# Head-pair stage of a hybrid decoder step: values one slot behind their transposes, one burst of projections a slot, low parts of weights on VectorE

## The chip, the cores and the metric

The kernel runs on one core of one Trainium2 chip. The metric is the device time of one execution in microseconds. Five engines work side by side: TensorE (PE), VectorE (DVE), ScalarE (ACT), GpSimd (POOL) and SyncE (SP), which here issues nearly all DMAs in one queue. Each runs its own instructions in the order written, and they meet only in semaphores.

## The reference

One inference step of a one-layer decoder, for a prompt of 16 + 1024 tokens and 8 running sequences with 2048 cached positions each. Cut to what matters here:

```python
n = rms_norm(x, g_mix)
q, k, v, xr, gr, gates = split(n @ w_in)
z = einsum(q, k) / 8 + bias                       # 16 heads, 4 key/value heads
tail = cumsum_from_the_right(log_sigmoid(-z) shifted by one)
attn = einsum(exp(log_sigmoid(z) + tail), v)      # masked to earlier keys
xc = causal_conv4(xr); h = rg_lru(xc, gates r and i)
x = x + (sigmoid(ga) * attn + sigmoid(gb) * h * gelu(gr)) @ w_out
x = x + conv_ffn(rms_norm(x, g_ffn))
```

For the 8 running sequences the same attention goes over pages of 128 cached keys and values, found by a page table.

## The kernel before

`phase_mix` is the stage that the diff touches. Its loop runs over 8 turns `i`, one for each pair of query heads, which is also one column tile of 128 channels of the recurrent branch and one running sequence of the decode attention. All engines run the same 17 slots a turn, `slots(i, first)`. Slot `s` stands for one block of 64 prompt queries (`BLOCK_ORDER` alternates long and short ones: block b has 16 + 64 b keys).

For one block the work passes from engine to engine: `scores` (PE, into `p_z`), `score_out` (ACT, copies it twice, to `sums` and `z`), softplus by Exp and Ln (ACT), `positive`, `summing` (a scan) and `argument` (DVE), `weights` (ACT, Exp), `turn` (PE, transposes of up to four key blocks, into `p_wt`), `turn_out` (DVE, to `w_t`), `values` (PE, into `p_av`), `values_out` (DVE). `turn` and `values` of a block run LAG = 3 slots behind its scores. A block's key blocks come in one to three groups of four (27 groups a turn).

The gaps of this chain on PE are filled with projections, `project_piece`: four weight tiles (xr, ga, gr, gb) of three chunks of 350 columns, each as three matmuls for each of 8 contraction tiles (high times high, high times low, low times high), and six gate matmuls on `xc`. `spread` cuts these into 102 pieces, 6 a slot, and each slot's six into three places: one ahead of `decode`, one between the first and second group of values, one behind `scores(i, s + 1)`. The chunks alternate between the two halves of `p_proj`; ACT copies a finished chunk at the end of its slot (L942), and a chunk may start when the one two before it is copied (`proj_out`).

The weight tiles are split into a high part by ACT (`high_part`, L868, in slots 1, 4, 8 and 12) and a low part by POOL (`low_part`, L852).

The tail of the recurrent branch of pair i - 1 runs in turn i: ACT does it in slot 0 (L918 to L920, with two changes of its table), ahead of the softplus of slot 0; DVE has `gate` and `late` in slots 0 and 3 to 6, and `conv` in slots 4, 6, 7, 8 and 11.

`decode` of one sequence runs in the same slots: in slots 0 to 7 PE transposes a pair of key pages into `p_kt` (L1209), ACT copies them (L914), and PE makes their scores a slot later (L1198); DVE takes the scores up in slot 8 to 10; in slots 12 to 15 two value steps each (L1224), with the value page as the stationary operand and 8 weight columns moving, into two places.

SP's order is written out (L790 to L831): for each turn q of slots 0 and 1, page pairs 0 and 1, k_in (which waits for the last scores of the turn before), q of slots 2 and 3, weights, gate weights, and then for s = 0 to 14 a q load, the page pairs of `PAGES_AT`, and at s = 2 the four loads of v (which wait for the last values of the turn before). A page pair may be loaded when the pair two before it has been used (`page_used`). Each page load reads two page numbers from the table into registers first (L772).

## Time and profile before

| | us |
|---|---|
| median of 3 runs | 2318.98 |
| lowest, highest | 2315.67, 2320.23 |
| the profiled execution's own time | 2312.59 |
| its span, first to last instruction | 2310.9 |
| busy PE, PE weight loads | 2027.3, 1825.2 |
| busy DVE, ACT, POOL | 1216.0, 936.3, 330.4 |
| mean granted TensorE clock | 0.934 of full |

Up to about 205 us the kernel makes q, k and v; the head-pair stage runs to about 1300 us; the rest is the output projection and the feed-forward part, which the change doesn't touch. Busy times are sums over the span. A row of a time line gives the start and the length of one instruction, or of several alike (x8) merged; matmul records overlap, so that their starts tell the pace, not their lengths. In square brackets stands how long the engine had been idle before it, and what ended that. A clock of 0.50 is 1.2 GHz, one of 1.00 is 2.4 GHz.

### The profile page before, as it was taken

Reading aid. Unit: us, or ns where it says so; the run is one execution under the profiler, and the core shown is the slowest. Engines: PE = TensorE matmul, PEld = TensorE weight load, DVE = VectorE, ACT = ScalarE, POOL = GpSimd, SP = SyncE. Lnnn points to the kernel's source line nnn. Section 1 sums busy time; section 2 is a strip of 40 time slices with the busy share of each in tenths; the row PEclk is TensorE's granted clock in tenths of the full one; section 3 lists DMA queues with packets and bytes.
Section 4 is the critical chain, followed back from the end, with each engine's and each line's share of the span. In section 5 each row is a group of like instructions: output and inputs, shape, how many; then the busy total and the mean of one; then the engine's idle time right before and its main releaser. Section 6 shows DMA issues by size and latency. Waiting matters only on the chain. (4 is left out here: it accounts for less than half of the span.)

```text
span 2310.9 us, 42010 instructions
## 1 busy us (share of the span) xinstructions
PE 2027.3 (88%) x14708; PEld 1825.2 (79%) x14708; DVE 1216.0 (53%) x2023; ACT 936.3 (41%) x1498; POOL 330.4 (14%) x150
## 2 busy tenths in 40 slices
PE   4996998979898897989989598899999999999986
PEld 3896876767677686767778476799999999999985
DVE  6100645647465664747566634455545555455555
ACT  4111656565655756566475612222211222112213
POOL 4121100000010000001000300322212222122210
PEclk9998988989889898989989799899999999999998
DMA  3233322131322213132221221111111111111104
GB/s 118 87 89 90 83 66 63 48 82 47 85 64 57 72 48 83 47 84 65 63 66 51 77 95 73 45 55 46 40 33 54 45 45 36 36 54 45 45 19 162
DMA packets 206433, 148.23 MB, mean 64 GB/s; under 512 B 66485, under 2 KB 194550, under 8 KB 206228
## 3 DMA queue, kind: packets, MB, share of 16 engines
q1 hardware_dynamic: 206254, 145.99, 21.8%
q8 instruction: 94, 1.54, 0.3%
q14 instruction: 85, 0.70, 0.1%
HBM read 128.57 MB, written 17.61 MB: 63 GB/s over the span
## 5 line engine op out<-in xcount | busy, mean ns | idle before, releaser
L87 PE MATMUL d_p_up<-n_hi,d_w_hi 128*128 128x350 f32 x1056 | 343.7, 325 | 14.0 <-POOL d_w_lo L1563 7.7
L87 PE MATMUL d_p_up<-n_lo,d_w_hi 128*128 128x350 f32 x1056 | 342.8, 325 | 0.0
L87 PE MATMUL d_p_up<-n_hi,d_w_lo 128*128 128x350 f32 x1056 | 342.6, 324 | 0.0
L1710 DVE TENSOR_TENSOR mix<-mix,d_p_down 128x350 f32<-128x350 f32 x264 | 137.3, 520 | 320.7 <-PE d_p_down L1757 320.7
L87 PE MATMUL b_p_proj<-n_hi,b_w_hi 128*128 128x350 f32 x768 | 304.8, 397 | 0.0
L1607 ACT ACTIVATE d_up<-d_p_up 128x350 f32<-128x350 f32 x132 | 60.8, 462 | 499.5 <-PE d_p_up L87 499.5
L87 PE MATMUL b_p_proj<-n_lo,b_w_hi 128*128 128x350 f32 x768 | 260.9, 340 | 0.0
L87 PE MATMUL b_p_proj<-n_hi,b_w_lo 128*128 128x350 f32 x768 | 260.4, 339 | 0.0
L974 DVE COPY b_w_t<-b_p_wt 128x512 f32<-128x512 f32 (+5 forms) x216 | 119.2, 552 | 246.0 <-PE b_p_wt L1171 245.1
L852 POOL TENSOR_TENSOR b_w_lo<-w_raw,b_w_hi 128x1024 fp32r<-128x1024 f32 x33 | 82.5, 2501 | 960.1 <-ACT b_w_hi L868 960.1
L87 PEld LDWEIGHTS d_p_up<-n_hi,d_w_hi 128*128 128x128 f32 x1056 | 200.6, 190 | 15.0 <-POOL d_w_lo L1563 8.1
L87 PEld LDWEIGHTS d_p_up<-n_hi,d_w_lo 128*128 128x128 f32 x1056 | 200.6, 190 | 0.0
L87 PEld LDWEIGHTS d_p_up<-n_lo,d_w_hi 128*128 128x128 f32 x1056 | 200.4, 190 | 0.0
L1563 POOL TENSOR_TENSOR d_w_lo<-w_raw,d_w_hi 128x1024 fp32r<-128x1024 f32 x45 | 114.3, 2550 | 516.5 <-ACT d_w_hi L1593 516.5
L87 PEld LDWEIGHTS b_p_proj<-n_hi,b_w_hi 128*128 128x128 f32 x768 | 155.6, 203 | 39.6 <-issue 29.5
L1757 PE MATMUL d_p_down<-d_a_hi,d_wd_hi 128*128 128x350 f32 x480 | 157.9, 329 | 23.7 <-DVE d_a_lo L1701 23.7
L995 DVE TENSOR_TENSOR_SCAN b_sums<-b_sums 128x720 f32<-128x720 f32 (+16 forms) x136 | 169.7, 1247 | 13.7 <-ACT b_sums L929 13.6
L891 ACT ACTIVATE b_sums<-b_p_z,b_bias 128x720 f32<-128x720 f32 (+16 forms) x136 | 94.6, 696 | 160.3 <-PE b_p_z L1158 160.2
L1186 PE MATMUL b_p_av<-b_w_t,b_v_in 128*64 128x64 f32 (+1 forms) x1440 | 83.6, 251 | 84.6 <-DVE b_w_t L974 84.2
L87 PEld LDWEIGHTS b_p_proj<-n_lo,b_w_hi 128*128 128x128 f32 x768 | 156.5, 204 | 1.7
L1757 PE MATMUL d_p_down<-d_a_hi,d_wd_lo 128*128 128x350 f32 x480 | 157.1, 327 | 0.0
L1757 PE MATMUL d_p_down<-d_a_lo,d_wd_hi 128*128 128x350 f32 x480 | 156.5, 326 | 0.0
(241 smaller groups left out, 4138.1 us busy)
## 6 DMA issues: line engine op xcount, KB each, us to landing
w_raw<-in_w_in SPq DMA_DIRECT2D x45, 512.0 KB, 4.5
w_raw<-in_w_up SPq DMA_DIRECT2D x45, 512.0 KB, 3.7
b_page<-in_cache_k SPq DMA_DIRECT2D x128, 128.0 KB, 2.1
b_page<-in_cache_v SPq DMA_DIRECT2D x128, 128.0 KB, 2.1
w_raw<-in_w_down SPq DMA_DIRECT2D x22, 512.0 KB, 3.2
b_q_in<-q_scr SPq DMA_DIRECT2D x272, 32.0 KB, 2.2
q_scr<-a_q_stage SPq DMA_DIRECT2D x16, 260.0 KB, 3.4
b_k_in<-k_scr SPq DMA_DIRECT2D x16, 260.0 KB, 4.0
```

What stands on the lines that cost most here:

```text
L87: last = pe.matmul(out, w[:, k, :], x[:, k, col:col + CW], start=(k == 0 and w is w_hi and x is x_hi), stop=(k == KT - 1 and w is w_lo))
L852: pool.tensor_tensor(w_lo[:, slot, :, :], w_raw[:, slot, :, :], w_hi[:, slot, :, :].bitcast(F32), ALU.subtract).then_inc(w_lo_ready, 1)
L891: own.mark(act.activation(so, pz, ACT.Abs, bias=bias[:, 0:1]))
L974: dve.tensor_copy(w_t[0:rows, at, 0:here, :], p_wt[0:rows, 0:here, :]).then_inc(wt_out, 1)
L995: dve.tensor_tensor_scan(pos[:, ::-1], so[:, ::-1], pos[:, ::-1], 0.0, ALU.add, ALU.add)\
L1186: last = pe.matmul(p_av[HD * a:HD * (a + 1), 0:QB], v[0:size, m, :], w_t[0:size, at, r, QB * a:QB * (a + 1)], start=(n == 0 and r == 0), s ...
L1563: pool.tensor_tensor(w_lo[:, slot, :, :], w_raw[:, raw, :, :], w_hi[:, slot, :, :].bitcast(F32), ALU.subtract).then_inc(lo_ready, 1)
L1607: act.activation(up[:, u % 2, CW * c:CW * (c + 1)], p_up[:, n % 2, 0:CW], ACT.Copy).then_inc(up_out, 1)
L1710: dve.tensor_tensor(to, to, p_down[:, n % 4, 0:CW], ALU.add).then_inc(down_out, 1)
L1757: last = pe.matmul(p_down[:, n % 4, 0:CW], w[:, k, P * tile:P * (tile + 1)], a[:, k, CW * c:CW * (c + 1)], start=(k == 0 and w is wd_hi an ...
```

## The change

- PE: in each slot first all `values` of the block four slots back, then up to two `turn` of the block three back, then all six projection pieces in one go, further `turn`, `decode`, and `scores(s + 1)` at the end. The transposed weights get four buffers in `w_t` instead of two, and two in `p_wt` instead of one.
- DVE: `turn_out` stands behind `summing`; the low parts move here from POOL, to the ends of slots 1, 4, 8 and 12.
- Decode: everything about a slot later (`V_STEPS` 13 to 16, `PAGES_AT` 13 to 15); ACT's copy of a key page pair moves one slot on, directly behind `score_out`. The value steps now take the decode weights (16 heads and 16 columns of zeros) as the stationary operand and 256 page columns as the moving one, into four groups of 32 rows; DVE copies the sums (`decode_sum_out`), and PE adds and picks them with eight small matmuls against `pick` in slot 1 of the next turn.
- PSUM: scores take two banks and 16 columns of `p_kt` instead of three banks; `p_av`, `p_pick` and the decode scores share `p_misc`.
- SP: the same order, with the v loads at s = 3 and the slot loop one longer.
- After the loop the run-out is written in slots as well.

```diff
-V_STEPS = {12: (0, 1), 13: (2, 3), 14: (4, 5), 15: (6, 7)}
-PAGES_AT = {**{s: (s + 2,) for s in range(8)}, 12: (10, 11), 13: (12, 13), 14: (14, 15)}
+V_STEPS = {13: (0, 1), 14: (2, 3), 15: (4, 5), 16: (6, 7)}
+PAGES_AT = {**{s: (s + 2,) for s in range(8)}, 13: (10, 11), 14: (12, 13), 15: (14, 15)}
...
-                    for s in range(SLOTS - 2):
+                    for s in range(SLOTS - 1):
...
-                        if s == 2:
+                        if s == LAG:
                             sp.wait_ge(av_group, nth(i, GROUPS, GROUPS - 1))
...
                         score_out(i, s, first)
+                        if 1 <= s <= 8:
+                            act.wait_ge(page_used, nth(i, 16, s - 1, 2))
+                            act.activation(k_t[:, :, :].rearrange("p a c -> p (a c)"), p_kt[:, :],
+                                           ACT.Copy).then_inc(kt_out, 1)
                         if not first or s >= 2:
                             weights(i, s - 2)
...
+                def low_part(slot, index):
+                    dve.wait_ge(w_hi_ready, index)
+                    dve.tensor_tensor(w_lo[:, slot, :, :], w_raw[:, slot, :, :],
+                                      w_hi[:, slot, :, :].bitcast(F32), ALU.subtract).then_inc(w_lo_ready, 1)
...
                         if u >= 0 or not first:
                             positive(i, u)
-                        if groups:
-                            turn_out(i, v, 0)
-                        if u >= 0 or not first:
                             summing(i, u)
-                        if groups > 1:
-                            turn_out(i, v, 1)
+                        for n in range(min(groups, 2)):
+                            turn_out(i, v, n)
                         if u >= 0 or not first:
                             argument(i, u)
-                        if groups > 2:
-                            turn_out(i, v, 2)
-                        if s == SLOTS - 1:
-                            decode_values_out(i)
+                        for n in range(2, groups):
+                            turn_out(i, v, n)
+                        if s in W_AT:
+                            low_part((W_AT.index(s) + 1) % 2, nth(i, 4, W_AT.index(s) + 1))
...
+                def pick_heads(i):
+
+                    pe.wait_ge(vd_copied, nth(i, 1, 0))
+                    for kv in range(KVH):
+                        for odd in range(2):
+                            last = pe.matmul(p_pick[HD * odd:HD * (odd + 1), 2 * kv:2 * kv + 2],
+                                             vacc[:, HD * kv:HD * (kv + 1)],
+                                             pick[:, 4 * kv + odd:4 * kv + odd + 3:2], start=True, stop=True)
+                    last.then_inc(vd_picked, 1)
...
+                        for n in range(2):
+                            m = 2 * j + n
+                            last = pe.matmul(p_vd[32 * (m % 4):32 * (m % 4 + 1), :], zd_wide[:, :, m],
+                                             page[:, j % 2, n, :], start=(m < 4), stop=(m >= PAGES - 4))
...
-                        if groups:
-                            turn(i, v, 0)
-                        for n in range(3):
-                            for piece in PLACES[s][n]:
-                                project_piece(i, *piece)
-                            if n == 0:
-                                decode(i, s)
-                            if n < groups:
-                                values(i, v, n)
-                            if n + 1 < groups:
-                                turn(i, v, n + 1)
-                            if n == 1 and s + 1 < SLOTS:
-                                scores(i, s + 1)
+                        for n in range(len(key_groups(unit(v - 1)[0])) if v >= 1 or not first else 0):
+                            values(i, v - 1, n)
+                        for n in range(min(groups, 2)):
+                            turn(i, v, n)
+                        for piece in PLACES[s]:
+                            project_piece(i, *piece)
+                        for n in range(2, groups):
+                            turn(i, v, n)
+                        decode(i, s, first)
+                        if s + 1 < SLOTS:
+                            scores(i, s + 1)
```

## Rows read from the trace of the kernel before

**Rows 1.** Windows view, one pass: us; busy PE, PEld, DVE, ACT, POOL; clock; DMA share; GB/s.
```profile
614.80:750.82 136.02, 118.84 (x1037) 98.83 (x1038) 79.86 (x135) 81.43 (x133) 10.40 (x4) 0.90 0.24 64
```

**Rows 2.** The waits of 210 to 1300 us: total, times, longest.
```profile
PE b_p_av L1186 <- DVE b_w_t L974: 90.5, 42, 7.1
...
PE b_p_z L1151 <- DMA b_k_in<-k_scr: 37.8, 6, 19.1
```

**Rows 3.** Time line of TensorE: start, us, line, what; idle before it.
```profile
342.15 1.48 PE L1151 MATMUL b_p_z<-b_k_in,b_q_in 64*64 64x360 f32 x8 [2.53 <-DMA b_k_in<-k_scr]
...
750.82 1.33 PE L1151 MATMUL b_p_z<-b_k_in,b_q_in 64*64 64x360 f32 x8 [4.02 <-issue]
...
768.40 1.12 PE L1186 MATMUL b_p_av<-b_w_t,b_v_in 128*64 128x64 f32 x16 [7.05 <-DVE b_w_t L974]
...
784.54 0.69 PE L1186 MATMUL b_p_av<-b_w_t,b_v_odd 128*64 128x64 f32 x16 [1.15 <-DMA b_v_odd<-v_scr]
...
801.17 0.69 PE L1186 MATMUL b_p_av<-b_w_t,b_v_in 128*64 128x64 f32 x16 [2.26 <-DVE b_w_t L974]
...
828.75 0.69 PE L1186 MATMUL b_p_av<-b_w_t,b_v_in 128*64 128x64 f32 x16 [1.59 <-DVE b_w_t L974]
```

**Rows 4.** The time line of ScalarE, same columns.
```profile
737.17 0.44 ACT L942 ACTIVATE r_gb<-b_p_proj 128x350 f32<-128x350 f32 x1
...
755.29 0.60 ACT L914 ACTIVATE b_k_t<-b_p_kt 128x512 f32<-128x512 f32 x1 [0.71 <-PE b_p_kt L1209]
...
771.28 0.53 ACT L892 ACTIVATE b_z<-b_p_z,b_bias 128x336 f32<-128x336 f32 x1
```

**Rows 5.** The time line of TensorE, work without a wait.
```profile
728.62 0.59 PE L1224 MATMUL b_p_z<-b_zd,b_page 128*128 128x8 f32 x4
...
733.30 0.27 PE L1158 MATMUL b_p_z<-b_never,b_ident_b 64*64 64x64 bf16 x2
...
758.02 0.33 PE L87 MATMUL b_p_proj<-n_hi,b_w_hi 128*128 128x350 f32 x1
758.18 0.33 PE L87 MATMUL b_p_proj<-n_lo,b_w_hi 128*128 128x350 f32 x1
...
772.46 0.89 PE L1151 MATMUL b_p_z<-b_k_in,b_q_in 64*64 64x392 f32 x8
...
776.59 0.63 PE L1209 MATMUL b_p_kt<-ident,b_page 128*128 128x128 f32 x4
```

**Rows 6.** The time line of SP's DMA issues.
```profile
322.50 3.12 SPq L777 DMA_DIRECT2D b_page<-in_cache_v  x4
...
337.31 1.14 SPq L798 DMA_DIRECT2D b_k_in<-k_scr  x2
...
729.75 3.10 SPq L777 DMA_DIRECT2D b_page<-in_cache_v  x4
...
740.51 3.23 SPq L777 DMA_DIRECT2D b_page<-in_cache_k  x4
...
744.05 1.14 SPq L798 DMA_DIRECT2D b_k_in<-k_scr  x2
...
777.40 0.87 SPq L777 DMA_DIRECT2D b_page<-in_cache_k  x2
...
780.25 0.38 SPq L826 DMA_DIRECT2D b_v_odd<-v_scr  x1
```

**Rows 7.** The time lines of GpSimd and VectorE.
```profile
825.17 2.40 POOL L852 TENSOR_TENSOR b_w_lo<-w_raw,b_w_hi 128x1024 fp32r<-128x1024 f32 x1 [28.22 <-ACT b_w_hi L868]
...
825.30 2.80 DVE L988 TENSOR_SCALAR b_sums<-b_z 128x976 f32<-128x976 f32 x1
...
843.53 1.23 DVE L1001 TENSOR_TENSOR b_z<-b_z,b_sums 128x1040 f32<-128x1040 f32 x1
```

**Rows 8.** TensorE, the products nearest to the new value steps.
```profile
835.53 0.59 PE L1215 MATMUL b_p_kt<-b_spd,tri 128*128 128x256 f32 x2
835.96 0.59 PE L1216 MATMUL b_p_kt<-b_laterd,ones 128*128 128x256 f32 x2
```

More of the change, by code:

```diff
@@ L526, with w_t_before, p_wt_at, p_wt_before @@
 GROUPS = GROUPS_TO[-1]
+W_T_AT = (0, 1, 2, 3, 0, 1, 2, 3, 0, 1, 2, 3, 0, 1, 2, 3, 0, 1, 2, 3, 0, 1, 2, 3, 0, 1, 2)
+assert len(W_T_AT) == GROUPS
+def w_t_before(q):
+    return q - next(k for k in range(1, GROUPS) if W_T_AT[(q - k) % GROUPS] == W_T_AT[q % GROUPS])
+def p_wt_at(q):
+    return q % GROUPS % 2
+def p_wt_before(q):
+    return q - (2 if q % GROUPS else 1)
 def group_of(s, n):
@@ L549, in spread @@
         assert all(n < GATE_FIRST for n, _, _ in here) or s >= 12
-        a = (len(here) + 2) // 3
-        b = a + (len(here) - a + 1) // 2
-        places.append([])
-        for part in (here[:a], here[a:b], here[b:]):
-            place = []
-            for n, k0, k1 in part:
-                if place and place[-1][0] == n and place[-1][2] == k0:
-                    place[-1] = (n, place[-1][1], k1)
-                else:
-                    place.append((n, k0, k1))
-            places[-1].append(place)
+        place = []
+        for n, k0, k1 in here:
+            if place and place[-1][0] == n and place[-1][2] == k0:
+                place[-1] = (n, place[-1][1], k1)
+            else:
+                place.append((n, k0, k1))
+        places.append(place)
     assert at == len(pieces)
@@ L701, in phase_mix @@
         ident_b = sb("b_ident_b", [P, P], BF16)
-        w_t = sb("b_w_t", [P, 2, 4, P])
+        w_t = sb("b_w_t", [P, 4, 4, P])
         xr, xc, gr, gb, rg, ig, pc, rc = (branch.xr, branch.xc, branch.gr, branch.gb, branch.rg, branch.ig,
@@ L756, in phase_mix @@
         masks = sem("b_masks")
-        passed = [sem(f"b_passed{s}") for s in range(3)]
+        passed = sem("b_passed")
         w_view = g.w_in.rearrange("o (k p) c -> p (o k) c", p=P)
@@ L845, in _ @@
                                    pattern=[[-1, P]], channel_multiplier=1).then_inc(inits, 1)
-                for n, (part, value) in enumerate(((gate_w[:, :, :], 0.0), (xc[:, LAST:COLS], 0.0), (zd[:, :, :], 0.0), (spd[:, :, PAGES:PAGES + 1], 0.0))):
+                for n, (part, value) in enumerate(((gate_w[:, :, :], 0.0), (xc[:, LAST:COLS], 0.0), (zd_wide[:, :, :], 0.0), (spd[:, :, PAGES:PAGES + 1], 0.0))):
                     pool.wait_ge(inits, n + 2)
                     pool.memset(part, value).then_inc(inits, 1)
-                def low_part(slot, index):
-                    pool.wait_ge(w_hi_ready, index)
-                    pool.tensor_tensor(w_lo[:, slot, :, :], w_raw[:, slot, :, :],
-                                       w_hi[:, slot, :, :].bitcast(F32), ALU.subtract).then_inc(w_lo_ready, 1)
-                low_part(0, 1)
-                with pool.Fori(0, KT, 1) as i:
-                    for t in range(4):
-                        low_part((t + 1) % 2, nth(i, 4, t + 1))
             @block.scalar
@@ L1115, in _ @@
                     if s == 0:
+                        decode_sum_out(KT)
                         positive(KT, -1)
@@ L1221, in decode @@
                         pe.wait_ge(page_arr[j % 2], 32 * nth(i, 8, 4 + j // 2))
-                        for pair in range(2):
-                            for n in range(2):
-                                last = pe.matmul(p_vd[pair], page[:, j % 2, n, P * pair:P * (pair + 1)],
-                                                 zd[:, 8 * pair:8 * (pair + 1), 2 * j + n],
-                                                 start=(j == 0 and n == 0), stop=(j == 7 and n == 1))
+                        for n in range(2):
+                            m = 2 * j + n
+                            last = pe.matmul(p_vd[32 * (m % 4):32 * (m % 4 + 1), :], zd_wide[:, :, m],
+                                             page[:, j % 2, n, :], start=(m < 4), stop=(m >= PAGES - 4))
                         last.then_inc(page_used, 1)
@@ L1271, in _ @@
                     slots(i, False)
-                for v in range(-LAG, 0):
-                    for n in range(len(key_groups(unit(v)[0]))):
-                        turn(KT, v, n)
-                        values(KT, v, n)
+                for s in range(LAG + 1):
+                    for n in range(len(key_groups(unit(s - LAG - 1)[0]))):
+                        values(KT, s - LAG - 1, n)
+                    for n in range(len(key_groups(unit(s - LAG)[0])) if s < LAG else 0):
+                        turn(KT, s - LAG, n)
+                pe.wait_ge(av_out, nth(KT, SLOTS, -1, 1))
+                pick_heads(KT)
 def phase_out(nc, g, branch, sem):
```

142 lines of the change are left out of this document (82 added, 60 removed).

## The prediction

> **What bounds the kernel now.** The span is 2310.9 us. I read the stage of the eight head pairs (one turn of the loop is called a pass here), because the diff touches nothing else. By the windows view one pass takes 136.02 us, with TensorE busy for 118.84, VectorE for 79.86 and ScalarE for 81.43, at a granted clock of 0.90 [rows 1]. TensorE carries the stage, and the other two matter where it waits for them. The list of waits has two large ones on TensorE: 90.5 us for `b_w_t` and 37.8 us for `k_in` (19.1 of them before the first pass) [rows 2]. The time line of one pass places them [rows 3]: 4.02 us at the loop boundary, 7.05 in slot 1, 1.15 in slot 3 (`v_odd`), and 2.26, 1.59 and two under half a microsecond later. That is some 17 us a pass. I ask of each whether it goes, and what is late next.
>
> **The stall of slot 1 hardly moves.** It looks like a wait for `w_t`, but behind it stands ScalarE. Call T the start of `scores(0)`, 750.82. ScalarE copies scores 0, then runs the whole tail of the pair before, and only then `score_out(1)`, which ends at 771.28 + 0.53 = T + 21.0 [rows 4]. In the changed kernel TensorE no longer waits for `w_t` there, but at the end of slot 1 stand `decode` (it waits for the k_t copy that ScalarE now makes behind `score_out(1)`) and `scores(2)` (waits for `z_copied`). The copy of slot 0, with its wait, leaves ScalarE's path: 0.71 + 0.60 [rows 4]. So `k_t` is there at T + 21.0 - 1.3 + 0.5 = T + 20.2; eight score products and four transposes follow, some 2 us at the low clock, and `scores(2)` starts at T + 22.2. Before it started at 772.46 (T + 21.6), with 6 projection matmuls of the slot still to do, which start 0.16 us apart (758.02, 758.18) [rows 5]. The gain is about 0.5 us, not 7. TensorE idles there about as long as now.
>
> **The loop boundary gets longer.** `k_in` is reloaded each pass, behind the first two pages of the next pair in SP's queue. SP works there as one chain with no wait visible in it: pages 14 and 15 at 729.75, loop jump, q loads, pages 0 and 1 at 740.51, `k_in` at 744.05, TensorE on at 750.82 [rows 3, 6]. That is 21.1 us from the issue of page 14; at the first boundary it is 342.15 - 322.50 = 19.65. I take 20.7. The chain starts when value step 4 has released its page: 728.62 + 0.59 = 729.21, 0.54 before the issue [rows 5, 6]. Today 17.6 us of TensorE's work lie between that step and the end of the pass (750.82 - 4.02 = 746.80), so only 4 us show. The change moves step 4 from the first third of slot 14 to the end of slot 15. What is left behind it: step 5, `scores(16)`, values of 5 key blocks, their 5 transposes, 15 projection matmuls and one gate, and steps 6 and 7, which I price from the rows at 0.7 + 0.5 + 0.9 + 0.5 + 3.1 + 1.3 = 7.0 us [rows 3, 5, 8] (16 value records in 0.69, projections 0.16 each, scores 0.89 for 392 columns of which these have 200). The gap becomes 0.54 + 20.7 - 7.0 = 14.2 us instead of 4.0: **+10.2 at each of 7 boundaries, +71**. Bounds: if SP's chain had 3 to 4 us of hidden waiting in it, the gap still is at least 8.7 (pages 0 and 1 can't be issued before steps 6 and 7; from 740.51 to 744.05 is 3.5, and from 337.31 to 342.15, the least from `k_in` to scores, 4.8, and the pair of page releases is 0.4 apart), so +4.7 to +11.5. ScalarE and VectorE can't use this time: their slot 0 stands behind `scores(0)`.
>
> **The v loads get late.** SP issues them behind pages 5 (before: pages 4), which wait for the page transposes of slot 3 (before: slot 2). Before, those transposes ended at 777.22, the page loads went at 777.40, the last v load at 780.25, and TensorE went on at 784.54: 7.3 us [rows 3, 5, 6]. In the changed kernel only `scores(4)` (about 1 us) lies between the transposes and the values that want v, since decode now closes the slot and values open the next. The stall is 6.3 us instead of 1.1: **+5.2 in each of 8 passes, +42** (bounds 4.5 to 6).
>
> **One burst of projections waits for its own copy-outs.** `p_proj` has two buffers, and the copies stand at the end of ScalarE's slot. In slot 15 the gate matmul rg 2 follows its predecessor's end directly. Before, `scores(15)` ended at 733.57 and the copy of that buffer at 737.61, 4.0 us later [rows 4, 5]; the new order brings TensorE there after 0.3 of values, 0.5 of transposes and 1.2 of projection: a stall of 2.0. The same in slot 13: 0.4. In slot 12 the first gate wants `xc`, whose last convolution on VectorE stands behind the scan of 1040 columns and behind `td_done`, now a slot later: 1.0 (0 to 2). For VectorE's slots that are fuller than TensorE's (4 and 9) 0.6. Together **+4.0 a pass, +32** (1 to 6 a pass).
>
> **What goes.** The later waits for `w_t`, since the copy now has a slot of time: 90.5 less 7 times 7.05 is 41, of which some 5 stand in the run-out behind the loop [rows 2, 3]: **-36**. The slot 1 term: **-4**. Clock: a pass at 0.90 holds some 27 us at half clock [rows 1] (0.1 lost of 136, twice over); 16 value matmuls take 1.12 us there and 0.69 at full clock [rows 3]. Two of the stretches (behind the 2.26 wait, behind the products of 8 columns) may go: 2.3 a pass, **-18** (0 to -40). Two restarts of the projections less a slot, 0.1 us at each edge less what other operations pay among themselves: 2.0 a pass, **-16** (0 to -27). The value steps: 16 products of 256 columns instead of 64 short records; the nearest row has 0.43 for such a product (two records, from 835.53 to 835.96) [rows 8], 6.9 a pass in series against 7.1 now, less where neighbours in other column groups overlap, and 0.3 to 1.8 for picking heads: 0.8 a pass, **-6** (+12 to -24).
>
> **Low parts on VectorE.** 33 subtractions of 1024 columns. No row has this one on VectorE; the nearest is a subtraction of 1040 columns, 1.23 us [rows 7], so 4.9 us a pass on an engine that is busy for 79.86 of 136. In return a GpSimd low part no longer holds it: one ran from 825.17 for 2.40 us, and the VectorE instruction of 825.30 took 2.80, though it goes over fewer columns than the subtraction of 1.23 [rows 7]. It is part of why `w_t` was late in slots 5 and 9. The instruction waits for ScalarE's high part, and behind it on VectorE stand the next slot's copies; with a slot of slack for `w_t` I cost this at nothing. If that cover were gone it would be up to 1.2 us four times a pass, 39 in all.
>
> By itself: the Trainium skill (SBUF — State Buffer, section "SBUF: two separate sides") says GpSimd and a VectorE operation of two SBUF inputs or a two-port mode hold one shared pair exclusively; the row of 2.80 us agrees, and by it the move is a gain, not a cost.
>
> **Sum.** 71 + 42 + 32 = 145 added, 36 + 4 + 18 + 16 + 6 = 80 removed, 1 for a longer run-out after the loop: +66. The profiled execution took 2312.6 us, so 2378.6; the median of the runs is 6.4 above it, so **2385 us**, 2.9% slower.
>
> **Rivals.**
> The clock falls (0.15). The short operations, today spread between three bursts, now stand together: decode, scores, values, transposes make 3 to 3.5 us without a projection. If the clock fell in two slots of a pass at 1.5 us each, and the gain of 2.3 did not come, that is 24 + 18 = 42 more, 2427. For it: a pass holds 27 us of half clock already. Against: scores and values run at full clock elsewhere. By itself: the Trainium skill (TensorE: Matmul & The Clock Gate, section "Part 4: PE-mode transpose") says that transposes don't count as activity for the gate; no row here separates them, and by that rule this rival would be likelier.
> VectorE becomes the bound (0.08). The low part waits, and the copies of `w_t` and the values' copy behind it come late: 39 more, 2424. Against: 80 us of 136.
> SP's chain has slack (0.12). The boundary costs +4.7 instead of +10.2: 39 less, 2346.
> Faster (0.08). The loads land as they do today, because a slot of SP's queue ahead makes up for both shifts, and only what goes counts: 32 - 80 = -48 gives 2271. It decides from the point where the page of step 4 is released more than 17 us ahead of the pass's end. Against: the order of SP's queue is unchanged there, and its releases move later.
> The change doesn't do what it says, the stalls stay and the loads cost nothing (0.04): about 2319.
> My forecast: 0.53, its own range 2350 to 2415.
>
> **Range and chances.** 2340 to 2430 leaves out the faster case, the unchanged one and the worst of the clock. Within 0.2% is about what a measurement of this kernel can tell from no change. Faster 0.08, same 0.04, slower 0.88, by the cases.
>
> **What would show it.** A gap of 12 to 16 us before `scores(0)` on TensorE, released by `k_in`, and pages 0 and 1 issued after the pass's last matmul; one of about 6 us before `values(0)` released by v; 6 to 8 us left in slot 1, released by ScalarE's `k_t`; some 2 us before the gate matmul of slot 15; no wait for `w_t` above 1 us; low parts on VectorE near 1.2 us. A boundary gap under 9 us, a v stall under 3 or a slot 1 stall under 3 would make it wrong.

## The result, and the profile after

The changed kernel takes 2360.32 us (median of 4 runs, 2354.44 to 2367.18), beside 2317.32 for the kernel before: a ratio of 1.0188, 95% interval 1.0155 to 1.0220. It is 43 us slower; the forecast was 2385 us in a range of 2340 to 2430. The profiled execution took 2354.44 us with a span of 2352.7, 41.8 more than before. The six inner passes grew from 135.3 us on average (342.15 to 1153.92) to 140.6 (349.34 to 1192.97), which makes 32 of it; the first pass, up to the boundary at its end, is 8.9 longer, and the remaining 1 lies ahead of it and in the eighth and what follows.

Windows view of the changed kernel, one pass, with the columns of [rows 1]:

```profile
629.77:769.51 139.74, 108.47 (x1021) 91.88 (x1022) 78.78 (x134) 82.01 (x135) 0.00 (x0) 0.88 0.24 63
```

TensorE is busy 10.4 us less than in [rows 1], and the pass is 3.7 us longer (the passes differ; the mean of the six is 5.3 longer). The waits of TensorE, 205 to 1340 us (total, times, longest), show where it stands instead; the first two lines of [rows 2] are `L1219 <- DVE b_w_t` and `L1181 <- DMA b_k_in` here:

```profile
PE b_p_z L1181 <- DMA b_k_in<-k_scr: 115.4, 8, 18.9
PE b_p_misc L1219 <- DMA b_v_odd<-v_scr: 42.0, 8, 5.4
PE b_p_misc L1247 <- ACT b_k_t L923: 30.7, 7, 4.4
PE b_p_misc L1229 <- DVE mix L1006: 19.7, 8, 3.7
PE b_p_proj L1286 <- ACT r_gb L957: 16.7, 8, 2.1
PE b_p_misc L1219 <- DVE b_w_t L998: 15.6, 19, 2.8
PE b_p_proj L1286 <- issue: 14.5, 8, 1.8
```

The time line of TensorE, from the boundary at 769.51 to the next slot 15, answers to [rows 3]:

```profile
769.51 1.48 PE L1181 MATMUL b_p_z<-b_k_in,b_q_in 64*64 64x360 f32 x8 [13.84 <-DMA b_k_in<-k_scr]
...
784.89 0.63 PE L1229 MATMUL b_p_misc<-b_pick,b_posd 128*64 128x2 f32 x16 [2.18 <-DVE mix L1006]
...
789.96 1.87 PE L1247 MATMUL b_p_misc<-q_block,b_k_t 128*128 x8 [4.44 <-ACT b_k_t L923]
...
813.34 1.55 PE L1219 MATMUL b_p_misc<-b_w_t,b_v_odd 128*64 128x64 f32 x24 [5.27 <-DMA b_v_odd<-v_scr]
...
851.84 1.43 PE L1219 MATMUL b_p_misc<-b_w_t,b_v_in 128*64 128x64 f32 x32 [0.89 <-DVE b_w_t L998]
...
866.60 0.83 PE L1286 MATMUL b_p_proj<-r_xc,b_gate_w 128*128 128x350 f32 x2 [1.82 <-issue]
...
887.50 0.85 PE L1286 MATMUL b_p_proj<-r_xc,b_gate_w 128*128 128x350 f32 x2 [2.10 <-ACT r_gb L957]
```

The boundary has gone from 4.02 to 13.84, v from 1.15 to 5.27; the 7.05 of slot 1 has become 2.18 and 4.44; the waits of 2.26 and 1.59 for `w_t` are 0.89 and less; slots 12 and 15 have new ones of 1.82 and 2.10. For the 1.82 the profile names no releaser, but VectorE's last convolution ends at 866.50, 0.10 ahead of the gate matmul at 866.60 that reads its `xc`:

```profile
865.21 1.29 DVE L1051 SCALAR_TENSOR_TENSOR r_xc<-r_xr,r_pc,r_xc 128x1040 f32<-128x1040 f32 x1
```

SP's issues around the boundary, beside [rows 6]:

```profile
750.14 3.10 SPq L800 DMA_DIRECT2D b_page<-in_cache_v  x4
...
756.55 3.11 SPq L809 DMA_DIRECT2D b_q_in<-q_scr  x4
761.21 3.21 SPq L800 DMA_DIRECT2D b_page<-in_cache_k  x4
764.73 1.14 SPq L821 DMA_DIRECT2D b_k_in<-k_scr  x2
```

and TensorE's value steps 4 to 7 in that pass (two steps a row):

```profile
748.94 0.67 PE L1273 MATMUL b_p_kt<-b_page,b_zd 128*32 128x256 f32 x8
...
754.64 1.03 PE L1273 MATMUL b_p_kt<-b_page,b_zd 128*32 128x256 f32 x8
```

The row of steps 4 and 5 ends at 749.61, and the last pages go 0.53 later. From the issue at 750.14 to the scores at 769.51 it is 19.4 us of one chain through SP, and TensorE has work for the first 6 (to 755.67).

**Where the time went, by TensorE's own accounts.** Add up the distances from start to start on TensorE over a pass, less the idle time in brackets, and a pass falls into work and waiting. Single passes, named by their starts:

| us a pass | before, 614.80 / 884.46 | changed, 629.77 / 911.43 | e7, 633.91 |
|---|---|---|---|
| idle | 17.2 / 16.6 | 31.2 / 31.6 | 27.8 |
| work | 118.9 / 119.1 | 108.6 / 109.7 | 113.3 |
| of it 288 projection matmuls | 57.9 / 58.1 | 50.8 / 51.1 | 57.1 |
| value steps and picking heads | 7.1 / 7.1 | 3.7 / 4.3 | 5.1 |
| prompt scores | 11.3 / 11.9 | 10.0 / 10.0 | 10.0 |

Waiting rose by 14.5 us, work fell by 9.8. The change is slower because waiting rose by more.

One pass differs from the next by several us in how much of its work fell into stretches at half clock (13.7 to 20.0 us in the changed kernel, 16.8 to 28.0 before). So here are the means of all six inner passes, and beside them the work with the clock taken out. That is an estimate: projection matmuls in the middle of a burst start 0.29 us apart at half clock and 0.16 at full, so 0.45 of the work at half clock is taken off, for all kinds of work alike.

| us a pass, mean of six | before | changed | e7 |
|---|---|---|---|
| idle | 17.0 | 31.8 | 27.3 |
| work | 118.3 | 108.8 | 113.6 |
| of it at half clock | 20.9 | 16.4 | 18.6 |
| work without the clock | 108.9 | 101.5 | 105.3 |
| of it 288 projection matmuls | 53.4 | 48.9 | 54.8 |
| value steps and picking heads | 7.1 | 3.9 | 3.8 |
| prompt scores | 8.9 | 8.9 | 8.8 |

Waiting rose by 14.8 and work fell by 9.5: 7.4 by the order and form of the work, 2.0 by the clock (rounded). The estimate holds together: e3, e4, e9 and e10, with the changed order and unlike amounts of work at half clock, come to 101.5 to 101.9. The prompt scores are the same work at a better clock. The mean granted clock of the pass is lower all the same (0.88 against 0.90), since it counts the waiting too.

### The profile page after: what moved, and what is told of

Its sections match the earlier page's. It is cut to its first block and busy times, and to the rows that moved or that the text cites. A ratio compares the mean times of both kernels' runs of the same rounds, so it can differ in the third digit from the quotient of the medians.

```text
span 2352.7 us, 41657 instructions
## 1 busy us (share of the span) xinstructions
PE 1956.7 (83%) x14580; PEld 1775.2 (75%) x14580; DVE 1209.6 (51%) x2020; ACT 940.9 (40%) x1514; POOL 247.9 (11%) x117
## 3 DMA queue, kind: packets, MB, share of 16 engines
q1 hardware_dynamic: 206254, 145.99, 21.3%
## 5 line engine op out<-in xcount | busy, mean ns | idle before, releaser
L87 PE MATMUL b_p_proj<-n_hi,b_w_hi 128*128 128x350 f32 x768 | 272.9, 355 | 0.0
L87 PE MATMUL b_p_proj<-n_lo,b_w_hi 128*128 128x350 f32 x768 | 253.7, 330 | 0.0
L87 PE MATMUL b_p_proj<-n_hi,b_w_lo 128*128 128x350 f32 x768 | 253.0, 329 | 0.0
L1006 DVE COPY mix<-b_p_misc 128x64 f32 (+2 forms) x136 | 29.8, 219 | 350.9 <-PE b_p_misc L1219 344.6
L1181 PE MATMUL b_p_z<-b_k_in,b_q_in 64*64 64x360 f32 (+16 forms) x1024 | 103.2, 466 | 115.4 <-DMA b_k_in<-k_scr 115.4
L87 PEld LDWEIGHTS b_p_proj<-n_lo,b_w_hi 128*128 128x128 f32 x768 | 151.0, 197 | 2.2
L87 PEld LDWEIGHTS b_p_proj<-n_hi,b_w_lo 128*128 128x128 f32 x768 | 149.9, 195 | 0.0
```

The costliest lines, as they stand in the source:

```text
L87: last = pe.matmul(out, w[:, k, :], x[:, k, col:col + CW], start=(k == 0 and w is w_hi and x is x_hi), stop=(k == KT - 1 and w is w_lo))
L1006: dve.tensor_copy(g.mix[:, bass.ds(i if s >= 0 else i - 1, 1), FIRST + q0:FIRST + q0 + nq] .rearrange("p a c -> p (a c)"), p_av[:, 0:nq]). ...
L1181: last = pe.matmul(banks[bank][QB * a:QB * (a + 1), 0:k1 - k0], q_in[rows, Q_AT[s], a, :], k_in[rows, k0:k1], start=True, stop=k1 <= diagonal)
```

## The experiments

Each was timed beside the kernel before on the same chip, and ratios are to it; the changed kernel was timed in another batch, so a difference to it is taken through the ratios and through the medians. Lengths of passes are means of the six inner ones, from one profile of each kernel.

**e1: the v loads ahead of the pages, in slot 3 of the changed kernel.**

```diff
-                        for j in PAGES_AT.get(s, ()):
-                            load_pages(i, j)
                         if s == LAG:
                             sp.wait_ge(av_group, nth(i, GROUPS, GROUPS - 1))
...
+                        for j in PAGES_AT.get(s, ()):
+                            load_pages(i, j)
```

> The changed kernel with SP's four v loads of slot 3 issued ahead of page pair 5. Theory (v comes late because its loads stand behind the page transposes of slot 3): the wait for v_odd, 5.1 to 5.4 us in each pass, falls under 1 us; 8 x 4.5 to 5.2, 36 to 42 us less than the changed kernel, so about 2320, ratio to before near 1.00. Rival (the wait is only slack that shows there; ScalarE and VectorE are as late): the gap moves to a wait for w_t or z in slots 4 to 6 and the time falls by less than 15 us.

2331.43 us, 1.0081 (1.0054 to 1.0108), some 27 us less than the changed kernel (25 by the ratios, 29 by the medians). TensorE's wait:

```profile
661.19 0.92 PE L1219 MATMUL b_p_misc<-b_w_t,b_v_odd 128*64 128x64 f32 x24 [1.45 <-DMA b_v_odd<-v_scr]
```

5.3 has become 1.45, 3.8 us eight times or 30, nearly all of it in the time (11.1 us of waiting for v are left of 42.0). The wait is caused by the place in SP's queue; the forecast of 36 to 42 assumed that it goes entirely.

**e2: `k_in` first in SP's pass; e3: both.**

```diff
+                    sp.wait_ge(qk_done, nth(i, SLOTS, SLOTS - 1))
+                    for half in range(2):
+                        sp.dma_start(k_in[HD * half:HD * (half + 1), :], g.k_scr[bass.ds(group, 1), :, :]
+                                     .rearrange("a p c -> p (a c)")).then_inc(k_arr, 16)
                     load_q(i, 0)
                     load_q(i, 1)
                     load_pages(i, 0)
                     load_pages(i, 1)
-                    sp.wait_ge(qk_done, nth(i, SLOTS, SLOTS - 1))
-                    for half in range(2):
-                        sp.dma_start(k_in[HD * half:HD * (half + 1), :], g.k_scr[bass.ds(group, 1), :, :]
-                                     .rearrange("a p c -> p (a c)")).then_inc(k_arr, 16)
```

> The changed kernel with SP's k_in loads as the first thing of a pass, ahead of q of slots 0 and 1 and of pages 0 and 1. Theory (the boundary is SP's chain): the gap before scores(0), 13.5 to 13.9 us, falls to about 6.3 (SP is back from its jump some 0.9 us after the pass's last matmul, and 5.4 from the k_in issue to the scores), so 7 x 7.5 = 53 us less, about 2307. Rival (TensorE's own jump and the landing of q take as long): the gap stays above 10, under 25 us less.

> Both orders of SP changed. If the two waits add up: 89 to 95 us less than the changed kernel, about 2267, ratio to before about 0.978: faster than both kernels. Rival (one wait hides the other, or they give way to ScalarE): less than 75% of the two gains together.

e2: 2314.38 us, 0.9996 (0.9978 to 1.0014), some 45 us less than the changed kernel. e3: 2281.42 us, 0.9863 (0.9830 to 0.9896), some 77 less; the two gains (27 and 45) add. The 53 and the 89 to 95 that were expected are missed, because neither wait went as far as forecast. The boundary in e2 and in e3:

```profile
614.36 1.48 PE L1181 MATMUL b_p_z<-b_k_in,b_q_in 64*64 64x360 f32 x8 [7.56 <-DMA b_q_in<-q_scr]
```

```profile
728.69 1.48 PE L1181 MATMUL b_p_z<-b_k_in,b_q_in 64*64 64x360 f32 x8 [6.99 <-DMA b_q_in<-q_scr]
```

The wait has halved and changed its releaser: behind `k_in` the q loads were next. With the boundary wait halved the changed kernel is level with the one before, with v shortened too it is ahead. These two waits are what makes it slower.

**e9: e3, with the next pass's q(0), q(1) and `k_in` issued ahead of SP's loop jump** (the last pass is written out behind the loop).

```diff
+                        if s in (12, 13) and more:
+                            load_q(i + 1, s - 12)
...
+                    if more:
+                        load_k(i + 1)
+
+                load_k(0)
+                load_q(0, 0)
+                load_q(0, 1)
+                with sp.Fori(0, KT - 1, 1) as i:
+                    one_pass(i, True)
+                one_pass(KT - 1, False)
```

> Both orders of SP as in the kernel with both loads ahead, and the next pass's q of slots 0 and 1 and k_in issued before SP's loop jump (k_in behind page 15, some 2.4 us ahead of the pass's last matmul). Theory: the gap before scores(0), 7.0 us there, falls to TensorE's own jump or k_in's landing, 3 to 4.5 us: 7 x 2.5 to 4 = 18 to 28 us less than 2281, about 2258. Rival (something else holds 7 us, such as SP's other loads behind it): under 8 us less.

2272.04 us, 0.9810 (0.9785 to 0.9834), 9 to 12 less than e3 where 18 to 28 were expected.

```profile
722.11 1.48 PE L1194 MATMUL b_p_z<-b_k_in,b_q_in 64*64 64x360 f32 x8 [3.82 <-issue]
```

The gap fell from 7.0 to 4.2 in the mean of the six (3.8 in this row), but a pass only from 130.3 to 129.4. What the boundary gives is lost again elsewhere: the work that TensorE does at half clock rose from 15.8 to 19.1 us a pass, and 0.45 of that rise is 1.5 of the missing 1.9 us. Why the clock fell more often isn't shown. The gap that is left isn't all TensorE's own, either, though the profile names no releaser: the second `k_in` load was issued at 716.37 and took 4.2 to land, so it landed at 720.56, 2.3 us after TensorE's last matmul had ended (718.28).

**e6 and e11: SP's order alone, in the kernel before.** e6 has the edit of e2; e11 also has the v loads ahead of the q load and the pages of slot 2.

> The kernel before with k_in as SP's first load of a pass; it waits there for the scores of slot 16, some 5.5 us ahead of the pass's end. k_in is then in place before the pass ends. Theory A (TensorE's own jump back takes near 4 us): the gap stays at 3.5 to 4.4 us and the time within 8 us of before. Theory B (k_in is what it waits for): the gap falls under 2 us, 14 to 28 us faster. Rival: q or the key pages come late now and the gap or slot 0 grows, slower.

> The kernel before with both edits of SP's order: k_in first in the pass, and the v loads of slot 2 ahead of that slot's q load and key pages. It tells how much of the time saved in the changed kernel by the same two edits (which took it from 2360 to 2281) the old order of work could have had too, and so what the new order of TensorE is worth once SP no longer holds it up. Theory (the new order gains by itself: projections and value steps faster, later waits for w_t gone): here only the boundary (worth 10 alone) and the v stall of 1.15 x 8 = 9 can go, so 2293 to 2301 us, ratio 0.990 to 0.994, and the kernel stays 12 to 20 us above the 2281 of the changed order with the same edits. Rival (the new order is worth nothing, the same edits give the same): 2285 or less, ratio 0.987 or below.

e6: 2303.32 us, 0.9956 (0.9939 to 0.9972). e11: 2289.79 us, 0.9898 (0.9876 to 0.9921). For e6 neither theory held: the gap fell to 2.2 to 2.7 us (A said 3.5 to 4.4, B under 2), and the time by 11 us. At the boundary there is a gap which no load ends:

```profile
739.43 0.83 PE L1151 MATMUL b_p_z<-b_k_in,b_q_in 64*64 64x360 f32 x8 [2.19 <-issue]
```

There `k_in` had landed a microsecond before TensorE's last matmul ended. The first boundary, where TensorE comes from the first turn, written out ahead of the loop, and doesn't jump back, has no such gap:

```profile
339.37 0.53 PE L1151 MATMUL b_p_z<-b_k_in,b_q_in 64*64 64x360 f32 x4 [0.47 <-DMA b_q_in<-q_scr]
```

So some 2.2 of the 4.02 in [rows 3] were TensorE's own jump, and only 1.8 were `k_in`. e11 lies below its forecast of 2293 to 2301 and above the rival's 2285. With like edits on SP the changed order (e3) has 0.9863 against 0.9898: ahead by 8 us, though the two intervals overlap, where I had expected 12 to 20. The new order is worth less by itself than its work suggests: of the six inner passes, e3 has 108.9 us of work against 116.0 in e11, but 21.3 of waiting against 15.7, above all since it still waits 6.99 at the boundary, where the old one waits 2.3.

**e7: the changed kernel with the six projection pieces of a slot in three places again** (before further `turn`, behind `decode`, behind `scores`).

```diff
-                        for piece in PLACES[s]:
+                        for piece in PLACES3[s][0]:
                             project_piece(i, *piece)
                         for n in range(2, groups):
                             turn(i, v, n)
                         decode(i, s, first)
+                        for piece in PLACES3[s][1]:
+                            project_piece(i, *piece)
                         if s + 1 < SLOTS:
                             scores(i, s + 1)
+                        for piece in PLACES3[s][2]:
+                            project_piece(i, *piece)
```

> The changed kernel with each slot's projection pieces in three places again (2 behind the transposes, 2 behind decode, 2 behind the next scores); values, transposes, copies and loads as changed. It sizes the one burst. As predicted (2.0 us a pass for the restarts, 4.0 lost to copy-outs in slots 12 to 15): the restarts come back, +16, the waits for the copy-outs mostly go, -20: within 15 us of the changed kernel. By the pace in the traces (288 projection matmuls took 57.9 us of a pass before and 51.3 after): if the burst makes all of that, +50 - 20, 20 to 35 us slower than changed; if the clock makes it, the pace stays at 51 to 53 us a pass and the time falls.

2361.88 us, 1.0198 (1.0175 to 1.0221): within 0.1% of the changed kernel. The tables above tell why that is a sum of two: over the six passes work is up by 4.8 and idle time down by 4.5. The same 288 matmuls take 57.1 us instead of 51.0 in the single passes, and 54.8 instead of 48.9 with the clock taken out. The trace has 47 bursts a pass in e7 (gate matmuls counted in) and 17 in the changed kernel, so 30 more breaks cost some 5.9 us, 0.20 each. The time came out as forecast, but by luck: the restarts cost 5.9 us a pass and not 2.0, and 4.5 less waiting (forecast 2.5) and 1.4 less for the transposes of key pages made up for it. The boundary shows one piece of it:

```profile
633.91 1.48 PE L1193 MATMUL b_p_z<-b_k_in,b_q_in 64*64 64x360 f32 x8 [12.04 <-DMA b_k_in<-k_scr]
```

Where TensorE waits for a chain elsewhere, slower work of its own costs nothing. Against e7's three places one burst is worth 6 us a pass, and as long as SP sets the boundary a good part of it isn't collected. Against the three places of the kernel before it is worth less: 53.4 to 48.9, some 4.4 us for 34 fewer bursts (51 to 17), 0.13 each. At full clock a projection matmul inside a burst starts 0.160 after the one before it in all three kernels; to the next start it takes 0.26 to 0.28 for the first of a burst, and for the last 0.20 before, 0.19 in the changed kernel and 0.24 in e7. So the price of a break depends on what follows it.

**e4, e5, e12: the low parts.** e4 is the changed kernel with `low_part` on GpSimd, e5 the kernel before with it on VectorE (at the ends of slots 1, 4, 8 and 12), e12 the fastest kernel (e10, below) with it on GpSimd. Each moves the same block, `low_part` and its calls; e5 in the direction opposite to the one shown:

```diff
-                def low_part(slot, index):
-                    dve.wait_ge(w_hi_ready, index)
-                    dve.tensor_tensor(w_lo[:, slot, :, :], w_raw[:, slot, :, :],
-                                      w_hi[:, slot, :, :].bitcast(F32), ALU.subtract).then_inc(w_lo_ready, 1)
+                def low_part(slot, index):
+                    pool.wait_ge(w_hi_ready, index)
+                    pool.tensor_tensor(w_lo[:, slot, :, :], w_raw[:, slot, :, :],
+                                       w_hi[:, slot, :, :].bitcast(F32), ALU.subtract).then_inc(w_lo_ready, 1)
```

> The changed kernel with the low parts of the projection weights back on GpSimd; all else as changed. My step priced this part at nothing, because w_t has a slot of time: within 6 us of the changed kernel (ratio to before 1.016 to 1.022). Rival (VectorE's low part is what keeps the w_t and xc waits, 0.9 + 0.6 + 1.8 us a pass): up to 15 us faster than changed. Rival (GpSimd holds VectorE for 2 us where it counts): slower by more than 10 us.

> The kernel before with one part of the change alone: the low parts on VectorE, at the ends of its slots 1, 4, 8 and 12. If GpSimd's 2.4 us hold on VectorE is part of why w_t came late (2.26 and 1.59 us in slots 5 and 9), those waits shrink by 1 us or more each and the time falls by 5 to 20 us (with the low parts back on GpSimd the changed kernel was 13 us slower). Rival (no slack for w_t in this order, so VectorE's own 1.23 us and its wait for the high part delay the transposes' copies): 10 to 30 us slower, with longer waits for w_t.

> The fastest kernel so far (2241 us, ratio 0.967) with the low parts of the weights back on GpSimd. In the changed kernel this alone cost 13 us, with the waits nearly the same and more time at the half clock. Theory A (GpSimd's 2.4 us operations slow VectorE's work, and TensorE's clock pays for it wherever VectorE is late): about 10 to 15 us slower here too, ratio 0.971 to 0.974. Theory B (the 13 us were the clock's reaction to the long idle stretches at the boundary and before values(0), which are gone here): within 5 us, ratio 0.965 to 0.969.

| | ratio (interval) | the part on VectorE against GpSimd |
|---|---|---|
| e4 | 1.0256 (1.0223 to 1.0290) | 12 to 16 us faster |
| e5 | 1.0077 (1.0053 to 1.0101) | 18 to 20 us slower |
| e12 | 0.9638 (0.9619 to 0.9657) | 7 to 11 us slower (the intervals of e10 and e12 overlap a little) |

In e5 the rival held, in e12 neither theory. In e4 the time is that of the last rival, but its mechanism isn't what happened, as the next rows show. The sign of the effect depends on the rest of the kernel.

The hold by GpSimd is real in the kernel before, where a GpSimd low part always met this instruction of VectorE; it is gone in the changed kernel, and does not come back in e4 (groups by form in the kernel before, the changed one and e4: total busy, mean ns, idle before):

```profile
L988 DVE TENSOR_SCALAR b_sums<-b_z 128x976 f32<-128x976 f32 x8 | 22.5, 2808 | 0.0
L1013 DVE TENSOR_SCALAR b_sums<-b_z 128x976 f32<-128x976 f32 x8 | 5.3, 660 | 0.0
L1016 DVE TENSOR_SCALAR b_sums<-b_z 128x976 f32<-128x976 f32 x8 | 5.2, 655 | 0.0
```

The sum of all VectorE instructions but the low parts tells what the hold costs VectorE in a pass: 85.4 before against 81.1 in e5, so 4.2; 80.6 in e4 against 80.2, so 0.4; 82.7 in e12 against 80.3 in e10, so 2.4. The time goes the other way: where the hold was largest, moving the low parts to VectorE cost most, and where there was next to none, it gained. e5 can be read. On VectorE the instruction itself is as priced, but it waits for ScalarE's high part (groups of VectorE: total busy, mean ns, idle before):

```profile
L958 DVE TENSOR_TENSOR b_w_lo<-w_raw,b_w_hi 128x1024 fp32r<-128x1024 f32 x33 | 40.4, 1226 | 73.0 <-ACT b_w_hi L858 73.0
```

(the changed kernel's low parts wait 29.1 in all), and behind it stand the copies of `w_t`, which have no slot of slack in the old order. TensorE in e5:

```profile
675.87 0.73 PE L1186 MATMUL b_p_av<-b_w_t,b_v_in 128*64 128x64 f32 x16 [3.19 <-DVE b_w_t L972]
...
704.75 0.69 PE L1186 MATMUL b_p_av<-b_w_t,b_v_in 128*64 128x64 f32 x16 [2.93 <-DVE b_w_t L972]
```

where [rows 3] have 2.26 and 1.59; the waits for `w_t` in all rose from 90.5 to 104.2. e12 against e10 is the same on a smaller scale: slot 1 waits for VectorE's `mix` 4.43 in e10 and 3.34 in e12, and the wait of 0.89 for `w_t` is gone:

```profile
720.46 1.02 PE L1243 MATMUL b_p_misc<-b_pick,b_posd 128*64 128x2 f32 x16 [4.43 <-DVE mix L1020]
```

```profile
720.08 1.02 PE L1244 MATMUL b_p_misc<-b_pick,b_posd 128*64 128x2 f32 x16 [3.34 <-DVE mix L1023]
```

e4 is the odd one. It waits 31.3 us a pass where the changed kernel waits 31.8, the 0.89 for `w_t` is gone, and yet a pass takes 142.9 instead of 140.6. The windows view has the difference in the clock:

```profile
636.48:779.51 143.03, 111.65 (x1021) 93.74 (x1022) 74.42 (x130) 82.23 (x135) 9.58 (x4) 0.86 0.23 61
```

The work done at half clock is 22.7 us a pass in e4 and 16.4 in the changed kernel. The difference of 6.3 costs 2.8 a pass (0.45 of it), which is the 2.3 and the half microsecond of shorter waits; without the clock the work is the same (101.5 in both). All four runs of e4 have it: their mean granted clock is 0.910 to 0.913, where the changed kernel has 0.917 to 0.922. Why the clock fell in more places I can't show. e12 speaks against a cause in GpSimd itself, for there it doesn't happen (11.8 in e12, 13.0 in e10).

**e8: the changed kernel with a shorter tail on ScalarE** (three of the gates' activations in slot 0 over 8 columns).

```diff
-        self.act_step(act, i, gr[:, :], gr[:, :], ACT.Gelu_apprx_tanh)
-        self.act_step(act, i, ga, ga, ACT.Tanh, scale=0.5)
-        self.act_step(act, i, gb[:, :], gb[:, :], ACT.Tanh, scale=0.5)
+        self.act_step(act, i, gr[:, 0:DEC], gr[:, 0:DEC], ACT.Gelu_apprx_tanh)
+        self.act_step(act, i, ga[:, 0:DEC], ga[:, 0:DEC], ACT.Tanh, scale=0.5)
+        self.act_step(act, i, gb[:, 0:DEC], gb[:, 0:DEC], ACT.Tanh, scale=0.5)
```

> The changed kernel with three of ScalarE's tail instructions of slot 0 (Gelu and two Tanh over 1050 columns, near 1.07 us each) cut to 8 columns; the rest of those three gates is left out of the result, and every wait stays. Theory (slot 1 is held by ScalarE's tail): about 2.6 us less until the k_t copy, so the two waits of slot 1 (2.2 and 4.4 us) lose 2.6 us together, 7 x 2.6 = 18 us less than changed, somewhat more in the run-out, 2335 to 2345. Rival (VectorE's w_t or its values' copy holds slot 1): the waits keep 6 us and the time falls by less than 6.

2352.12 us (the median of two runs), 1.0143 (1.0117 to 1.0170), 9 us less than the changed kernel, where 18 or more were expected.

```profile
643.98 0.63 PE L1229 MATMUL b_p_misc<-b_pick,b_posd 128*64 128x2 f32 x16 [1.10 <-DVE mix L1006]
...
649.05 1.87 PE L1247 MATMUL b_p_misc<-q_block,b_k_t 128*128 x8 [4.43 <-ACT b_k_t L923]
```

The pass of these rows starts at 631.20, so TensorE goes on at T + 17.85 instead of T + 20.45 (789.96 less 769.51): 2.6 us earlier, as the chain on ScalarE says. That slot 1 hangs on ScalarE's tail is thereby shown. The wait for `mix`, 19.7 us in all in the changed kernel, is nearly gone:

```profile
PE b_p_misc L1229 <- DVE mix L1006: 2.3, 3, 1.1
```

The passes became only 1.2 us shorter (139.4). Idle time fell by 2.3 a pass, nearly the forecast 2.6, but work rose by 1.1, and work at half clock rose from 16.4 to 18.4, which is 0.9 of it. Why the clock fell more often isn't shown.

**e10: e9 with the v loads ahead of the slot's q load too, and the gate matmuls of slots 13 and 15 that wait for a copy put behind decode.**

```diff
+BEFORE_DECODE = {13: 2, 15: 2}
...
-                        for piece in PLACES[s]:
+                        now = BEFORE_DECODE.get(s, len(PLACES[s]))
+                        for piece in PLACES[s][:now]:
                             project_piece(i, *piece)
...
                         decode(i, s, first)
+                        for piece in PLACES[s][now:]:
+                            project_piece(i, *piece)
```

> The kernel with loads ahead of SP's jump, and two more edits: the v loads ahead of the slot's q load too, and in slots 13 and 15 the pieces from the gate matmul on that waits for a copy of its own slot stand behind decode. Theory: the v wait of 1.4 to 1.6 us goes, and of the 2.10 us of slot 15 and what slot 13 loses some 1.5; 8 x 2.5 to 3 = 20 to 24 us less than 2272, about 2250, ratio to before 0.972. Rival (half clock or a new wait takes it, as it took two thirds of the shorter boundary gap there): under 8 us less.

2240.83 us, 0.9668 (0.9648 to 0.9688); e12, with the low parts on GpSimd, 2229.54 us, 0.9638. Both beat the kernel before (by 3.3 and 3.6%) and the changed one. The wait for v in the loop and the one of slot 15 are gone, and at the boundary about the jump of TensorE is left (1.4 to 2.6 us; `k_in` lands between 0.3 ahead of the last matmul's end and 0.6 behind it):

```profile
705.74 0.83 PE L1195 MATMUL b_p_z<-b_k_in,b_q_in 64*64 64x360 f32 x8 [1.44 <-issue]
```

Other waits took part of their place, for the value pages above all (4.9 us in e9):

```profile
PE b_p_kt L1287 <- DMA b_page<-in_cache_v: 20.2, 15, 1.8
```

A pass takes 124.9 us, 15.7 less than in the changed kernel; the time is 31 to 33 us under e9, where 20 to 24 were expected. By the passes most of it is the clock: waiting fell by 1.8 us a pass, and work at half clock from 19.1 to 13.0, which is 2.7 a pass or 22 in eight. Whether the calmer queue or the moved matmuls did that isn't parted.

## Why the prediction was right, and where its sizes were off

**The waits were right to the sum, partly by luck.** Predicted, a pass waits 10.2 + 5.2 + 4.0 more and 4.5 + 0.5 less, so 14.4; the tables have 14.5 and 14.8. The large waits are there and are ended as forecast, but v was put 1.1 too high and the later waits for `w_t` 1.3 too high, and these two cancel. One by one:

- Boundary, 14.2 against 13.84. The terms, from the end of the row of steps 4 and 5: 0.53 to the issue (forecast 0.54), 19.4 of chain (20.7), 6.1 of work behind it (7.0, in which step 5 was counted). Two errors of a microsecond cancel. The chain was read too long at 750.82, where by e6 some 2 us of the jump of TensorE itself stand in the gap; the first boundary, without a jump, had 19.65. Pages 0 and 1 went at 761.21, after the last matmul, as forecast. e2 shows the cause, and the rival of slack in SP's chain is out.
- v, 6.3 against 5.27. The last v load went at 810.19, TensorE on 3.15 later, where before it took 4.29 (780.25 to 784.54); the distance was taken whole from one row of before, where this load took 4.2 from issue to landing and here 3.0. Why it lands faster isn't shown. e1 shows the cause of the wait.
- Slot 1, `k_t` and the scores at T + 20.2 against T + 20.45, released by ScalarE as said; e8 shows the cause. The split in two waits, the first by picking heads for VectorE's `mix`, was not foreseen.
- Slot 15, 2.0 against 2.10; slot 12, 1.0 (0 to 2) against 1.82, ended by `xc` as said, going by the times; slot 13, nothing against 0.4.
- No wait for `w_t` above 1 us in the loop: the longest are 0.89 and 0.56; the 2.8 is in the run-out. In all 15.6 us of the 41 are left, so 25 went and not 36, 3.2 a pass and not 4.5.

**The work was under-priced as a gain.** Predicted were 2.3 + 2.0 + 0.8 = 5.1 us a pass, measured 9.8 in the single passes and 9.5 in the mean of six. Two terms were mis-sized. The restarts of the projections: 2.0 became 4.4 (53.4 to 48.9 without the clock). I had taken 0.1 us at each edge and put most of that against what the other operations pay among themselves; a break costs 0.13 altogether. e7 shows that the one burst is the cause, though its three places cost more than those of before, 5.9. The value steps with their picks: 0.8 became 3.3 (7.13 to 3.86). I took two records of 256 columns, 0.43 apart in [rows 8], as serial; in the new form neighbours go into other column groups, and four products (eight records) are over in 0.67 (748.94) or 1.03 (754.64), where in series they would take 1.7. The clock term came near its forecast, but one profile can't carry that far: over six passes work at half clock fell from 20.9 us a pass to 16.4, which is 2.0 against the 2.3 forecast; over the last four of them it fell from 19.8 to 16.9, which is 1.3, and e4 shows how easily such a term moves. The other kinds of work come to nothing together (values 0.9 less, their transposes 1.1 more, without the clock).

So an inner pass grew by 5.3 us where 9.3 were forecast. In six passes that is 24 us, all of the distance between the forecast for the profiled execution (2378.6) and its 2354.4.

**Low parts on VectorE** were costed at nothing because `w_t` has a slot of slack. The instruction lasts 1.23 (forecast 1.2). e5 shows the cost without that cover, 18 us, within the bound of 39. With it, e4 says a gain of 12 to 16, e12 a loss of 7 to 11. So the term was small as said, but its sign can't be given for the order alone. The Trainium skill (SBUF — State Buffer, section "SBUF: two separate sides") says that GpSimd and a VectorE operation with two SBUF inputs or in a two-port mode hold one shared pair exclusively. The hold itself is in the rows (2.80 in [rows 7], 0.66 for the same instruction in the changed kernel), but the gain that the prediction read from it did not follow: it was largest in the kernel before, and there the move cost 18 us. In e5 what decides is where the instruction stands in VectorE's order, and in e4 the clock; for e12 it isn't shown.

**The rivals.** TensorE did less work at half clock in the changed kernel than before (16.4 us a pass against 20.9), so the rule that transposes don't count for the clock (the Trainium skill, TensorE: Matmul & The Clock Gate, section "Part 4: PE-mode transpose") does not show in this change; it was not tested apart. VectorE did not become the bound: 78.78 of 139.74. SP's chain had no slack. The loads did not land in time as the faster rival had it; where they are moved ahead, in e3, e9 and e10, the changed order gives 2281 to 2241, around the 2271 of that rival.

## What to carry to other kernels

When work that releases a buffer is moved later, follow the queue of loads behind that release to the end of the loop turn, and count what work of the consumer is left after it: here 6 us of work against a chain of 20. A reordering can make its engine's work much cheaper and still lose; look for the one or two waits that eat it and move their loads ahead in the queue, which here turned 1.019 into 0.986 and then 0.967. Price an edit in the order in which it will stand: the same few lines cost 18 us in one kernel, brought 12 to 16 in the next and cost 7 to 11 in the third. And take the clock out before you price a kind of work from two traces: here it held a fifth of the work that was saved.

## What the runs showed of the hardware

- TensorE's own jump to the next loop turn costs 2.2 to 2.7 us in e6, with `k_in` and q landed half a microsecond or more ahead, and 1.4 to 1.8 in those passes of e10 where `k_in` landed just ahead of the last matmul's end. At the first boundary of e6, without a jump, the gap is 0.47.
- A burst of 350-column matmuls that is broken by short products costs 0.13 us (before against changed) to 0.20 us (e7) for each break at full clock: the first matmul of a burst takes 0.26 to 0.28 to the next start, the last 0.19 to 0.24, one inside 0.160. At half clock one inside takes 0.29, not twice 0.16.
- Four products with 32 columns stationary and 256 moving, each in its own column group, were over in 0.67 and in 1.03 us at full clock; one of 128 columns by 256 took 0.43 to the start of the next [rows 8].
- A VectorE instruction over 976 columns took 2.81 us beside a GpSimd subtraction and 0.66 without it (before, changed), yet taking the hold away made the kernel before 18 us slower (e5), since what came in its place stood in the way.
- The same work may cost more by the clock alone: e4 and the changed kernel differ by 6.3 us a pass of work at half clock, with like waits.
